# The z projection, the order inside differential attention, and the rule that hands out PSUM banks

## The reference

```python
def even_mixer(h, cos, sin, w_in, ...):
    qkv_a, z_a, b_a, a_a, q_b, k_b, v_b = split_cols(h @ w_in, EVEN_SPLITS)   # 1536, 512, 4, 4, 512, 512, 512
    qkv_a = silu(causal_conv(qkv_a, conv_w))
    ...
    o_a = gated_delta_rule(q_a, k_a, v_a, g, beta)
    o_a = rms_norm(o_a, gdn_norm_w) * silu(z)
    ...
    o_b = diff_attention(q_b, k_b, v_b, lam)          # 4 heads, 2 maps of 64 per head, v of 128
    return concatenate([o_a, rms_norm(o_b) * (1 - lambda_init)]) @ w_out

def block(start):                                     # 128 query rows of a head
    s = einsum('bhmqd,bhmkd->bhmqk', qb, kh)          # m = 2 maps
    a = softmax(where(causal, s, -1e30))
    a = a[:, :, 0] - lam * a[:, :, 1]
    return einsum('bhqk,bhkd->bhqd', a, vh)
```

## Time and profile before

| | us |
|---|---|
| median of 3 runs | 3998.58 (3994.32 to 4002.80) |
| the profiled execution, its span | 4002.8, 4000.6 |
| PE busy | 3497.8 (87%) |
| DVE busy | 2078.6 (52%) |
| ACT busy | 1325.5 (33%) |
| diff stage, PE's first matmul to that of the next stage | 66.0 |
| PE's granted clock, mean | 0.92 |

### The profile page before, as it was taken

How to read it: one execution, slowest core, us unless ns; L and a number is a source line. 1 busy time by engine, 2 the same in 40 slices (tenths; PEclk the granted TensorE clock), 3 DMA queues, 4 the chain that set the end, 5 groups by cost and what they waited for, 6 DMA issues and landing times.

```text
span 4000.6 us, 50517 instructions
## 1 busy us (share of the span) xinstructions
PE 3497.8 (87%) x20714; PEld 2724.3 (68%) x20714; DVE 2078.6 (52%) x3581; ACT 1325.5 (33%) x2152; POOL 363.1 (9%) x338
## 2 busy tenths in 40 slices
PE   6987899999998999996987999668787778998998
PEld 4757677776785777774766766456666666776886
DVE  5444456654324466545355255566766673444443
ACT  3242232222223322232331234354444442423321
POOL 0002100000000000000000000143333330000000
PEclk9888899999898999998888799878988888999999
DMA  3210024433440244422111200211111101232221
GB/s 128 59 50 1 6 92 134 128 121 73 70 100 11 74 127 135 129 74 90 43 53 38 85 27 22 69 40 36 30 36 30 43 15 64 64 126 74 95 95 64
DMA packets 318852, 274.89 MB, mean 69 GB/s; under 512 B 10912, under 2 KB 310048, under 8 KB 317856
## 3 DMA queue, kind: packets, MB, share of 16 engines
q1 hardware_dynamic: 314368, 256.07, 21.6%
q10 hardware_dynamic: 4256, 15.59, 1.1%
HBM read 265.35 MB, written 6.29 MB: 68 GB/s over the span
## 4 chain that ended last, share of the span: by engine, by line
PE 71%; DVE 16%; ACT 6%; issue 3%; POOL 2%; DMA 1%; DVEq 0%; ACTq 0%; POOLq 0%; SPq 0%
PE ps L89 70%; DVE f L101 5%; DVE f L95 4%; DVE r L95 3%; DVE f L107 2%; ACT f L82 2%; POOL f L95 2%; PE ps L92 2%; ACT L82 1%; ACT f L86 1%; DVE f L98 1%; ACT r L86 1%; DVE f L104 0%; ACT f L83 0%; DVE r L101 0%
## 5 line engine op out<-in xcount | busy, mean ns | idle before, releaser
L89 PE MATMUL ps<-r,r 128*128 128x512 f32 (+3 forms) x10656 | 2543.4, 398 | 146.3 <-DVE r L95 96.4
L89 PEld LDWEIGHTS ps<-r,r 128*128 128x128 f32 x10656 | 2013.9, 197 | 628.4 <-issue 196.1
L89 PE MATMUL ps<-f,f 64*64 64x64 f32 (+7 forms) x9122 | 896.2, 289 | 292.3 <-DVE f L95 77.1
L89 PEld LDWEIGHTS ps<-f,f 64*64 64x64 f32 (+3 forms) x9122 | 628.6, 169 | 541.2 <-issue 179.4
L95 DVE TENSOR_TENSOR r<-f,r 128x1024 fp32r<-128x1024 f32 (+2 forms) x619 | 662.1, 1076 | 537.8 <-ACT r L86 530.7
L86 ACT ACTIVATE r<-f 128x1024 fp32r<-128x1024 f32 (+2 forms) x548 | 507.0, 937 | 853.6 <-PE ps L89 715.3
L86 ACT ACTIVATE f<-ps 128x512 f32<-128x512 f32 (+3 forms) x418 | 189.4, 463 | 706.4 <-PE ps L89 482.1
L101 DVE SCALAR_TENSOR_TENSOR f<-f,f,f 128x128 f32<-128x128 f32 (+3 forms) x630 | 363.2, 583 | 70.2 <-ACT f L82 54.1
L95 POOL TENSOR_TENSOR f<-f,f 128x512 f32<-128x512 f32 (+2 forms) x280 | 319.4, 1155 | 615.1 <-ACT f L82 403.7
L95 DVE TENSOR_TENSOR f<-ps,f 128x512 f32<-128x512 f32 (+4 forms) x325 | 178.1, 561 | 327.1 <-PE ps L89 318.2
L82 ACT ACTIVATE f<-ps 128x512 f32<-128x512 f32 (+4 forms) x202 | 113.3, 563 | 645.4 <-PE ps L89 643.3
(11 more groups left out here) (32 smaller groups left out, 718.7 us busy)
## 6 DMA issues: line engine op xcount, KB each, us to landing
f<-in_w_mlp_up SPq DMA_DIRECT2D x32, 1024.0 KB, 6.5
f<-in_w_mlp_down SPq DMA_DIRECT2D x32, 1024.0 KB, 6.5
f<-in_w_ff SPq DMA_DIRECT2D x32, 1024.0 KB, 5.3
f<-in_w_ada SPq DMA_DIRECT2D x48, 512.0 KB, 4.0
f<-in_w_in SPq DMA_DIRECT2D x24, 1024.0 KB, 5.3
f<-in_w_in SPq DMA_DIRECT2D x44, 512.0 KB, 3.8
f<-in_w_in_even SPq DMA_DIRECT2D x12, 1024.0 KB, 5.5
f<-in_w_in_odd SPq DMA_DIRECT2D x12, 1024.0 KB, 12.1
```

The lines of the kernel that those rows point to most:

```text
L89: return self.e.matmul(out, l, r, start=first, stop=last)
```

## The change

It has three parts. The z projection leaves the differential-attention stage: its four tiles are whole tiles right behind q/k/v, and ACT applies Silu as it reads them out of PSUM. The attention stage gets four phases instead of six: scores; maxima and exponentials; normalisation, transposes and the copy of the transposed block; product with v and the copy of the result, 128x128 per unit. Copies are shared: for even units DVE copies the transposed block and ACT the result, for odd units the other way round. All engines go through a round with the older units first. `Psum` hands out banks by a pointer that goes round and passes over banks that are held.

```diff
     def __init__(self, banks):
-        self.t, self.free = banks, list(range(8))
-        self.drained = [[] for _ in banks]
-
-    def hold(self, pe, *drained):
-        b = self.free.pop(0)
+        self.t, self.next = banks, 0
+        self.drained, self.open = [[] for _ in banks], [False] * 8
+
+    def take(self, pe, *drained):
+        while self.open[self.next]:
+            self.next = (self.next + 1) % 8
+        b = self.next
+        self.next = (b + 1) % 8
         for name, value in self.drained[b]:
             pe.wait_ge(name, value)
         self.drained[b] = list(drained)
         return b
 
+    def hold(self, pe, *drained):
+        b = self.take(pe, *drained)
+        self.open[b] = True
+        return b
+
     def leave(self, b):
-        self.free.append(b)
-
-    def take(self, pe, *drained):
-        b = self.hold(pe, *drained)
-        self.leave(b)
-        return b
+        self.open[b] = False
...
         for n in range(12):
             G.tile(pe, ("even.qkv", n), W, n * 128, 128, X, [("ev_pad", n + 1)])
+        for n in range(4):
+            G.tile(pe, ("even.z", n), W, 1536 + n * 128, 128, X, [("ev_z", n + 1)])
...
-        for u, p in waves(16, 6):
+        for u, p in waves(16, 4):
             h, qt = self.units[u]
             if p == 0:
-                if u < 8:
-                    G.half(pe, ("even.z", u // 2), self.W, 1536 + u // 2 * 128, X, [("ev_z", u // 2 + 1)], u % 2)
...
-            elif p == 3:
+            elif p == 2:
                 pe.wait_ge("diff_a", u + 1)
-                b = self.bank["t", u] = K.ps.take(pe, ("diff_pt", u + 1))
+                b = self.bank["t", u] = K.ps.take(pe, ("diff_pt" + "da"[u % 2], u // 2 + 1))
...
-            elif p == 4:
-                pe.wait_ge("diff_pt", u + 1)
-                if qt == 0:
-                    self.bank["o", h] = K.ps.hold(pe, ("diff_o", h + 1))
+            elif p == 3:
+                pe.wait_ge("diff_pt" + "da"[u % 2], u // 2 + 1)
+                b = self.bank["o", u] = K.ps.take(pe, ("diff_o" + "ad"[u % 2], u // 2 + 1))
...
@@ ACT @@
+        for n in range(4):
+            G.act(act, ("even.z", n))
+            act.wait_ge("mm", K.done["even.z", n])
+            act.f(self.z[:, n, :], G.at["even.z", n], ACT.Silu).then_inc(S("ev_z"), 1)
...
-            elif p == 3:
+            elif p == 2 and u % 2:
                 act.wait_ge("mm", K.done["diff.t", u])
                 if u >= 3:
                     act.wait_ge("mm", K.done["diff.o", u - 3])
-                act.cp(self.pt[u % 3][:, 0:km], K.ps.t[self.bank["t", u]][:, 0:km]).then_inc(S("diff_pt"), 1)
-            elif p == 5 and qt == 3:
+                act.cp(self.pt[u % 3][:, 0:km], K.ps.t[self.bank["t", u]][:, 0:km]).then_inc(S("diff_pta"), 1)
+            elif p == 3 and not u % 2:
                 act.wait_ge("mm", K.done["diff.o", u])
...
-        act.wait_ge("ev_z", 4)
-        for n in range(4):
-            act.f(self.z[:, n, :], self.z[:, n, :], ACT.Silu).then_inc(S("ev_zs"), 1)
...
@@ DVE @@
-        for u, p in ((r - p, p) for r in range(21) for p in (1, 2, 0) if 0 <= r - p < 16):
+        for u, p in waves(16, 4):
...
                 dve.stt(scs[0][:, 0:km], scs[1][:, 0:km], cols[1][:, 0:1], scs[0][:, 0:km], MUL, ADD).then_inc(S("diff_a"), 1)
+                if not u % 2:
+                    dve.wait_ge("mm", K.done["diff.t", u])
+                    if u >= 3:
+                        dve.wait_ge("mm", K.done["diff.o", u - 3])
+                    dve.cp(self.pt[u % 3][:, 0:km], K.ps.t[self.bank["t", u]][:, 0:km]).then_inc(S("diff_ptd"), 1)
+            elif p == 3 and u % 2:
+                dve.wait_ge("mm", K.done["diff.o", u])
+                dve.cp(self.o[:, 4 + h, qt * 128:km], K.ps.t[self.bank["o", u]][:, 0:128]).then_inc(S("diff_od"), 1)
```

More of the change, by code:

```diff
@@ L17 @@
 STAGES = (
-    {"ev_pad": 12, "ev_padz": 3, "ev_conv": 12, "ev_qkv": 12, "ev_ba": 4, "ev_y": 1, "ev_na": 1, "ev_beta": 1, "ev_rope": 8,
-     "ev_dv": 4},
-    {"diff_elam": 1, "diff_exp": 32, "ev_z": 4, "diff_pt": 16, "diff_o": 4, "ev_zs": 4, "diff_lam": 2, "diff_max": 32,
-     "diff_a": 16},
+    {"ev_pad": 12, "ev_padz": 3, "ev_conv": 12, "ev_qkv": 12, "ev_z": 4, "ev_ba": 4, "ev_y": 1, "ev_na": 1, "ev_beta": 1,
+     "ev_rope": 8, "ev_dv": 4},
+    {"diff_elam": 1, "diff_exp": 32, "diff_oa": 8, "diff_pta": 8, "diff_lam": 2, "diff_max": 32, "diff_a": 16, "diff_ptd": 8,
+     "diff_od": 8},
     {"gdn_expR": 4, "gdn_DTe": 4, "gdn_ekdf": 4, "gdn_ebE": 4, "gdn_y0": 12, "gdn_y1": 12, "gdn_NW": 4, "gdn_o": 4,
@@ L975, in diff_pe @@
     def diff_pe(self, pe):
-        K, G, X = self.K, self.K.G, self.norm.X
-        for u, p in waves(16, 6):
+        K = self.K
+        for u, p in waves(16, 4):
             h, qt = self.units[u]
@@ L996, in diff_pe @@
                 K.mm_done(t, ("diff.t", u))
-            elif p == 4:
-                pe.wait_ge("diff_pt", u + 1)
-                if qt == 0:
-                    self.bank["o", h] = K.ps.hold(pe, ("diff_o", h + 1))
-                b = self.bank["o", h]
+            elif p == 3:
+                pe.wait_ge("diff_pt" + "da"[u % 2], u // 2 + 1)
+                b = self.bank["o", u] = K.ps.take(pe, ("diff_o" + "ad"[u % 2], u // 2 + 1))
                 for kt in range(qt + 1):
-                    t = pe.mm(K.ps.t[b][:, qs], self.dv[:, kt, h * 128:h * 128 + 128], self.pt[u % 3][:, kt * 128:kt * 128 + 128],
-                              qt + kt == 0, qt + kt == 6)
+                    t = pe.mm(K.ps.t[b][:, 0:128], self.dv[:, kt, h * 128:h * 128 + 128], self.pt[u % 3][:, kt * 128:kt * 128 + 128],
+                              kt == 0, kt == qt)
                 K.mm_done(t, ("diff.o", u))
-                if qt == 3:
-                    K.ps.leave(b)
     def gdn_pe(self, pe):
@@ L1124, in diff_act @@
         act.f(lam[:, 0:2], lam[:, 0:2], ACT.Exp).then_inc(S("diff_elam"), 1)
-        for u, p in waves(16, 6):
+        for u, p in waves(16, 4):
             h, qt = self.units[u]
             km = (qt + 1) * 128
-            if p == 0 and u < 8:
-                k = ("even.z", u // 2)
-                self.K.G.act(act, k)
-                if u % 2:
-                    act.wait_ge("mm", K.done[k])
-                    act.cp(self.z[:, u // 2, :], self.K.G.at[k]).then_inc(S("ev_z"), 1)
-            elif p == 1:
+            if p == 1:
                 for m in range(2):
@@ L1142, in diff_act @@
                     act.wait_ge("mm", K.done["diff.o", u - 3])
-                act.cp(self.pt[u % 3][:, 0:km], K.ps.t[self.bank["t", u]][:, 0:km]).then_inc(S("diff_pt"), 1)
-            elif p == 5 and qt == 3:
+                act.cp(self.pt[u % 3][:, 0:km], K.ps.t[self.bank["t", u]][:, 0:km]).then_inc(S("diff_pta"), 1)
+            elif p == 3 and not u % 2:
                 act.wait_ge("mm", K.done["diff.o", u])
-                act.wait_ge("mm", K.done["even.z", 3])
-                act.cp(self.o[:, 4 + h, :], K.ps.t[self.bank["o", h]][:, :]).then_inc(S("diff_o"), 1)
-        act.wait_ge("ev_z", 4)
-        for n in range(4):
-            act.f(self.z[:, n, :], self.z[:, n, :], ACT.Silu).then_inc(S("ev_zs"), 1)
+                act.cp(self.o[:, 4 + h, qt * 128:km], K.ps.t[self.bank["o", u]][:, 0:128]).then_inc(S("diff_oa"), 1)
     def gdn_act(self, act):
@@ L1192, in dve @@
             t.then_inc(S("ev_conv"), 1)
+        for n in range(4):
+            G.dve(dve, ("even.z", n))
         G.dve(dve, ("even.ba", 0, 0))
@@ L1258, in diff_dve @@
             scs = [self.sc[(2 * u + m) % 6] for m in range(2)]
-            if p == 0 and u < 8:
-                K.G.dve(dve, ("even.z", u // 2))
-            elif p == 1:
+            if p == 1:
                 if u >= 3:
```

## The result

The changed kernel takes 4072.6 us (median of 4 runs, 4068.71 to 4075.57), the kernel before 4000.7 in runs on the same chip: a ratio of 1.0175 (95% interval 1.0148 to 1.0202), 72 us slower. The forecast was 4050 with a range to 4070. The direction and the three places were right; the sum was 22.6 us too small.

A forecast was written before the change was run, and what follows sets the result against it. PE held 71% of the chain of waits, DVE 16%. 4002.8 + 23.8 + 10.2 - 1.3 + 17.8 + 1 = 4054.3 us profiled, 4050 on the median; eight in ten from 4026 to 4070.

The forecast's parts named there:

- z: q/k/v section: z's 96 matmuls of 128x512 join PE's back-to-back work there, +23.8 us.
- the three places: Where time was to be added: q/k/v section +23.8, differential-attention stage +10.2, RWKV's reuse of PSUM banks +17.8 us.
- The tables: Start of the next stage: the load of Exp is not needed now, -1.28 us.
- The stage at full clock: Differential-attention stage laid out anew without z: 16.6 us for four units instead of 8.65, +4.7 us in all.
- odd units' copies behind PE's product: Differential attention: DVE's copy of O stands ahead of the normalisation; the steps take 3.93 and 4.21 us.
- the exposed exponentials: Differential attention: nothing lies between maxima and normalisation, exposing 1.04 us for 512 columns, 0.8 estimated for 256.
- The charge for the clock: Differential-attention stage: PE's pieces 1.46 times as long at the lower clock, +10.8 us in all, half charged, +5.5.
- Rival C: Low clock through the whole differential-attention stage, RWKV at its upper end: 4056 to 4063 us; chance 0.20.
- The banks: PSUM ring: a bank just left may be taken next; +17.8 us in RWKV and +1 at NSA's output.
- Sparse attention: NSA's output: once, a bank just left is the next take, +1 us.
- RWKV's 15 units: RWKV: banks of units 2, 4, 6, 8 and 10 are reused early, 5 x 3.55 = 17.8 us, bounds 0 and 25.
- the forecast's 3.55: RWKV: x2 waits for rw_out of the same round, delaying the dense half and DVE, +3.55 us, five times.

## Why the forecast was too low

- **z.** In nine executions with z moved the stage starts at 273.7 us on the mean, in eight without at 250.3: +23.4, the forecast 23.8. The profiled execution's 25.4 has 2 us of chance in it.
- **The tables.** Right: the load is gone, and ACT's first function of the next stage starts 2.59 us behind PE's first matmul instead of 3.87, 1.28 less. The -1.5 of the whole stretch says little, since its first part varies from 1638.8 to 1644.3 between kernels that differ only in the stage ahead of it.
- **The stage at full clock.** 16.3 us per head, worked out as 16.6. The waits were the right ones: odd units' copies behind PE's product, then the exposed exponentials. But I took the second for a cost that could be undone by itself. It can't, with four phases: the kernels with the maxima first (85.7 and 74.1) show that the tight loop from a normalisation through transposes and scores to the next maxima takes its place. One phase more gives 24.4 us back, by the depth and, in a part that was not separated, by the clock that rises with it; the order of maxima and normalisation then gives 5.8.
- **The charge for the clock.** This step failed. I charged half of 10.8 us, 1.35 per head. The clock stood at 0.50 in nearly all windows, so the whole was due; and 1.46 was too small a factor for PE's pieces. It came from 1.42 us for a product with v of four blocks at full clock, twice the price of two blocks, where the product takes 1.16: the factor is 1.8, and scores of 512 columns, from 0.57 to 1.04, have the same. Measured, the clock is 3.8 us per head, 15 in the stage where 5.5 were charged. Rival C had this stage right in kind. The Trainium skill ("TensorE: Matmul & The Clock Gate", on depth-cycling of the PSUM queue as a second failure of the gate) says that PE which idles shortly between groups swings between its two clocks. The loss agrees, the swinging hardly: in this stage the clock stayed low but for 3.4 us, and it swung more (0.50 to 0.84 in windows of 10 us) in the kernels whose stage was shorter.
- **The banks.** +30.3 against 18.8. Sparse attention, up to RWKV's first products: 336.7 us behind its fence before, 339.8 after, +3.2, forecast +1; which of the reuses there carries it was not tried, and one kernel with the list also had 340.2, one with the ring 336.5. RWKV's 15 units: 669.1 and 693.9, +24.8, forecast 17.8. The end: +2.4, forecast 0. The wait was foreseen instruction by instruction; this term's price failed. The working had 0.6 us for x5 and x2 and 3.03 for the half. x2 takes 1.09 at full clock (2845.32 to 2846.41 above), so of the 3.1 us missing in the round shown some 0.5 is under-priced work, and the rest is the clock: PE, idle for 5.77 us, does x2 in 1.92 and the half in 4.86. Against this the kernel before was itself slow in places where the ring isn't. Its products at the head of a unit, and after:

```profile
2947.52 1.99 PE L89 MATMUL ps<-f,f 64*64 64x128 f32 x32 [1.45 <-DVE f L95]
```

```profile
2948.27 1.10 PE L89 MATMUL ps<-f,f 64*64 64x128 f32 x32 [1.46 <-DVE f L95]
...
3004.84 1.10 PE L89 MATMUL ps<-f,f 64*64 64x128 f32 x32 [1.93 <-DVE f L95]
```

Of the five even units concerned, before's second, third and fourth start like this one with products of 1.99, the first and the fifth with 1.10; after, all take 1.10. By pairs of units the ring costs 7.1, 3.7, 3.7, 3.5 and 7.9: dear where the kernel before had been at full clock, cheap where it had not. That the three middle pairs meet the forecast's 3.55 is luck, one slowness set against another.

## What to carry to other kernels

Count phases by what an engine finds in its queue: when the consumer of a result stands in the same round as its producer on another engine, every round waits for the loop, and reordering inside the round gives nothing. A bank or buffer that was held must not be handed out again before its last reader is likely done; a free list that appends at its end does this by itself, a ring needs it told. And where a change puts long waits between PE's groups, work the sum out with PE's pieces at the lower clock throughout as well, each by a row of its own at either clock.

## What the runs showed of the hardware

With PE working in stretches of up to 4.3 us between waits of mostly 0.8 to 2.2 us, the granted clock was 0.50 in nearly all of 85 us; seven matmuls of 128x512 more per round (1.86 us) brought it to 1.00, and with the old order of the stage it was 1.00 without them. At the lower level, float32 products of 64x512 and the product with v of four blocks took 1.8 times as long (1.04 and 0.57, 2.07 and 1.16), three transposes 1.6 times (0.90 and 0.55); 12 dense matmuls of 128x512 took 4.86 instead of 3.03 with the clock granted at 0.57. One idle time of 5.77 us in RWKV was followed by 6.6 us of slow work. Filling that idle time moved the slow part behind the next idle time. Twice a table load of 1.28 us had no idle time of ACT behind it (the Silu at 454.06, and the first Silu 0.02 us behind the load at 312.14 in the kernel before).
